# An expert layer's outputs: summed by matrix products in PSUM, or scattered to DRAM by row and gathered by token

## What is computed

```python
def hier_moe(h, router_grp, router_grp_b, router_exp, router_exp_b, w_gate, w_up, w_down):
    # top-1 group of 4, then top-2 experts of the 8 inside that group; 32 SwiGLU experts of width 256
    ...
    w_top = jax.nn.softmax(top_logit, axis=-1) * p_grp
    ...
    for grp in range(N_GROUPS):
        hid = silu(einsum('td,edf->tef', t, w_gate[grp])) * einsum('td,edf->tef', t, w_up[grp])
        out = out + einsum('tef,efd->td', hid * combine[:, grp, :, None], w_down[grp])

h_lat = h_lat + m_lat[5] * hier_moe(modulate(rmsnorm(h_lat, norm_ffn_g), ...), ...)
out = rmsnorm(h_lat, final_norm_g)
```

## Time and profile before

| | us |
|---|---|
| median of 3 runs | 2294.93 |
| the profiled execution's own time | 2294.58 |
| its span, first to last instruction | 2292.7 |
| PE busy in the span | 2112.8 (92%) |
| first matrix product of the pairs | at 1982.66 |
| end of the last combining product | at 2273.76 |
| mean granted TensorE clock | 0.953 of full |

### The profile page before, as it was taken

The page is one execution under the profiler, slowest core; times in us unless marked ns, Lnnn a source line. Parts: engine busy times, 40 slices in busy tenths (PEclk is TensorE's granted clock), DMA queues, the critical chain, the costliest instruction groups (busy, mean ns, idle before and its releaser), DMA issues. The chain is left out here.

```text
span 2292.7 us, 36330 instructions
## 1 busy us (share of the span) xinstructions
PE 2112.8 (92%) x15874; PEld 1296.2 (57%) x15874; DVE 798.8 (35%) x1625; ACT 512.7 (22%) x1042; POOL 101.1 (4%) x103
## 2 busy tenths in 40 slices
PE   6989999999999999999998887899988997799996
PEld 3545568854445658864544776885488643333332
DVE  1474323211185323310245446436344413311112
ACT  2223322201114413210121332123331201211111
POOL 0000000000000000000000011000012000000000
PEclk9999999999999999999998988899999998899998
DMA  6351325533343236334211000100110163298881
GB/s 260 146 201 56 145 110 220 221 147 147 127 187 139 104 124 257 147 147 155 92 43 51 3 3 2 48 13 37 74 40 3 45 258 131 97 391 349 351 347 59
DMA packets 30507, 313.87 MB, mean 137 GB/s; under 512 B 4744, under 2 KB 7184, under 8 KB 9488
## 3 DMA queue, kind: packets, MB, share of 16 engines
q1 hardware_dynamic: 28048, 308.40, 34.3%
q0 software_dynamic: 2304, 3.15, 0.4%
HBM read 330.39 MB, written 3.16 MB: 145 GB/s over the span
## 5 line engine op out<-in xcount | busy, mean ns | idle before, releaser
L511 ACT ACTIVATE arena<-pair 128x512 f32<-128x512 f32 (+5 forms) x339 | 181.0, 547 | 698.7 <-PE pair L885 170.6
L1262 PE MATMUL pair<-arena,weight_ring 128*128 128x256 f32 x1408 | 310.5, 383 | 2.9 <-ACT arena L785 2.9
L885 PE MATMUL pair<-weight_ring,arena 128*128 128x512 f32 (+1 forms) x640 | 277.0, 586 | 19.1 <-issue 11.3
L1262 PEld LDWEIGHTS pair<-arena,weight_ring 128*128 128x128 f32 x1408 | 269.7, 192 | 43.7 <-issue 6.8
L885 PEld LDWEIGHTS pair<-weight_ring,arena 128*128 128x128 f32 x640 | 122.9, 195 | 155.6 <-issue 150.1
L1308 PE MATMUL pair<-weight_ring,arena 128*128 128x512 f32 x352 | 151.5, 592 | 3.1 <-DVE arena L1282 3.1
L1282 DVE SCALAR_TENSOR_TENSOR arena<-pair,columns,arena 128x255 f32<-128x255 f32 (+1 forms) x176 | 76.7, 477 | 201.8 <-ACT arena L1273 200.3
L1308 PEld LDWEIGHTS pair<-weight_ring,arena 128*128 128x128 f32 x352 | 66.8, 190 | 86.7 <-issue 83.2
L1568 PEld LDWEIGHTS pair<-arena 64*64 64x64 f32 x3584 | 111.9, 140 | 4.4 <-issue 3.7
L1568 PE MATMUL pair<-arena 64*64 64x64 f32 x3584 | 113.8, 224 | 0.0
L1382 PE MATMUL pair<-weight_ring,arena 128*128 128x512 f32 (+1 forms) x256 | 106.5, 574 | 4.5 <-DVE arena L704 4.5
(11 more groups left out here) (473 smaller groups left out, 2642.1 us busy)
## 6 DMA issues: line engine op xcount, KB each, us to landing
weight_ring<-stream SPq DMA_DIRECT2D x85, 2048.0 KB, 7.4
weight_ring<-experts_in SPq DMA_DIRECT2D x17, 2048.0 KB, 10.3
arena<-experts_in SPq DMA_DIRECT2D x15, 2048.0 KB, 11.6
arena<-experts_out SPq DMA_DIRECT2D x8, 2048.0 KB, 14.3
weight_ring<-experts_out SPq DMA_DIRECT2D x8, 2048.0 KB, 13.2
weight_ring<-stream SPq DMA_DIRECT2D x4, 1024.0 KB, 4.8
arena<-rows_in SPq DMA_DIRECT2D x1, 3264.0 KB, 21.8
weight_ring<-stream SPq DMA_DIRECT2D x2, 1152.0 KB, 5.1
```

What stands on the lines that cost most here:

```text
L511: copy_act = lambda dst, src: nc.scalar.activation(dst, src, ACT_F.Copy)
L885: last = mm(bank[b][:, 0:n], hT[:, k, m * P:(m + 1) * P], w[:, k * n:k * n + n], start=(j == 0), stop=(j == KD - 1))
L1262: last = mm(bank[b][:, j * S:(j + 1) * S], w[:, at:at + P], hT[:, k, :], start=(k == 0), stop=(k == KD - 1))
```

## The change

The products with C and the factors spread over it are gone. A table `places_i` of row numbers is formed instead by DVE (`sorted_rows`), with one column for each pair and four columns for the tokens. ACT and DVE copy the down product out as before, without a factor, and POOL then scatters the 128 rows of Y, 4 KB each, to a DRAM tensor `y_dram` at their sorted places (`rows_out`). Slots with no row of work are sent to one of 16 spare rows if they lie on partitions 0 to 15, and out of bounds if not. Each scatter waits for the one before, and a Y buffer is written again once the scatter of two pairs earlier has landed. After the last scatter POOL gathers, for each of the two tiles of 128 tokens, the row of its first and of its second expert (four indirect DMAs of 512 KB). DVE multiplies them by gate factor and modulation row and adds them to the residual; then norm, gain and store run by tile. PSUM banks 2 to 5 take the down products in turn. The extra pairs move to places 5, 9, 13 and 17.

```diff
         starts_i = sb("window_starts", [P, 40], mybir.dt.int32)
+        places_i = sb("sorted_places", [P, 24], mybir.dt.uint32)
         rows_i = sb("extra_rows", [P, 8], mybir.dt.uint32)
         bias_dram = nc.dram_tensor("bias_rows", (HEADS, 2 * S - 1), F32, kind="Internal").ap()
+
+        y_dram = nc.dram_tensor("sorted_outputs", (2 * S + 16, D), F32, kind="Internal").ap()
 
...
             pair_windows = [2 * i for i in range(N_EXP // 2)]
-            for at, w in ((3, 32), (8, 34), (13, 36), (18, 38)):
+            for at, w in ((5, 32), (9, 34), (13, 36), (17, 38)):
...
-            for b, values, out_ in ((0, slots2, posT), (1, w12, wT)):
...
+            def sorted_rows():
+
+                link(tt(picked, taken_by, by_slot(ends), ALU.mult))
+                link(nc.vector.tensor_reduce(limits[:, N_EXP:N_EXP + 8], picked, AX, ALU.add))
+                nc.vector.tensor_copy(limits[:, 0:N_EXP], ends)
+                nc.vector.tensor_scalar(row_at[0:CH], firsts[0:CH, 0:40:2], k3c("slot", 1)[0:CH], None, ALU.add)
+                nc.vector.tensor_scalar(row_spare, k3c("slot", 1), k3c("skip", 1), 2.0 * S, ALU.subtract, ALU.add)
+                link(nc.vector.tensor_scalar(row_at[CH:P], firsts[CH:P, 1:40:2], k3c("slot", 1)[CH:P], -float(CH),
+                                             ALU.add, ALU.add))
+                tt(row_ok[0:CH], row_at[0:CH], limits[0:CH, 0:40:2], ALU.is_lt)
+                link(tt(row_ok[CH:P], row_at[CH:P], limits[CH:P, 1:40:2], ALU.is_lt))
+                link(nc.vector.scalar_tensor_tensor(row_at, row_at, row_spare, row_ok, ALU.subtract, ALU.mult))
+                link(nc.vector.tensor_scalar(row_at, row_at, row_spare, None, ALU.add))
+                nc.vector.tensor_copy(places_i[:, 0:20], row_at)
+                return nc.vector.tensor_copy(places_i[:, 20:24], place2.rearrange("p c m -> p (c m)"))
+            places_mark = dve_after(sorted_rows, ("dve", c.dve))
...
-            def combine_weights(i):
...
-                    link(nc.vector.scalar_tensor_tensor(parts_, posT, k3c("slot", 1, at), wT, ALU.is_equal, ALU.mult))
-                    tt(C, parts_[:, 0, :], parts_[:, 1, :], ALU.add).then_inc(dve_done, 1)
...
-                hT, Y = hTs[i % 2], Ys[i % 2]
+                hT, Y, ob = hTs[i % 2], Ys[i % 2], 2 + 2 * (i % 2)
                 if PE:
                     PE.wait_ge(act_done, hidden_done[i])
-                    if i >= 1:
-                        PE.wait_ge(act_done, left_done[i - 1])
-                        PE.wait_ge(dve_done, right_done[i - 1])
+                    if i >= 2:
+                        PE.wait_ge(act_done, left_done[i - 2])
+                        PE.wait_ge(dve_done, rows_done[i - 2])
                 w = await_expert(3 * i + 2)
...
-                                last = mm(bank[2 + h_][CH * j:CH * j + CH, :], hT[:, t, CH * j:CH * j + CH],
+                                last = mm(bank[ob + h_][CH * j:CH * j + CH, :], hT[:, t, CH * j:CH * j + CH],
...
                     if i >= 2:
-                        ACT.wait_ge(pe_done, combined[i - 2])
-                    nc.scalar.activation(Y[:, 0, :], bank[2][:, :], ACT_F.Copy).then_inc(act_done, 1)
+                        ACT.wait_ge(y_sent, 16 * (i - 1))
+                    copy_act(Y[:, 0, :], bank[ob][:, :]).then_inc(act_done, 1)
                 c.act += 1
                 left_done[i] = c.act
                 if DVE:
                     DVE.wait_ge(pe_done, outputs_done[i])
                     if i >= 2:
-                        DVE.wait_ge(pe_done, combined[i - 2])
-                    nc.vector.tensor_copy(Y[:, 1, :], bank[3][:, :]).then_inc(dve_done, 1)
+                        DVE.wait_ge(y_sent, 16 * (i - 1))
+                    nc.vector.tensor_copy(Y[:, 1, :], bank[ob + 1][:, :]).then_inc(dve_done, 1)
                 c.dve += 1
-                right_done[i] = c.dve
-
-            def combine(i):
-
-                C, Y = Cs[i % 2], Ys[i % 2]
-                if PE:
-                    PE.wait_ge(dve_done, max(weights_done[i], right_done[i]))
-                    PE.wait_ge(act_done, left_done[i])
-                    for m in range(TT):
-                        for h_ in range(2):
-                            last = mm(bank[4 + 2 * m + h_][:, :], C[:, P * m:P * m + P], Y[:, h_, :],
-                                      start=(i == 0), stop=(i == npairs - 1))
-                    last.then_inc(pe_done, 1)
-                c.pe += 1
-                combined[i] = c.pe
+                rows_done[i] = c.dve
+
+            def rows_out(i):
+
+                at = pair_windows[i] // 2
+                if POOL:
+                    POOL.wait_ge(dve_done, rows_done[i])
+                    POOL.wait_ge(act_done, left_done[i])
+                    if i:
+                        POOL.wait_ge(y_sent, 16 * i)
+                    POOL.indirect_dma_start(out=y_dram, out_offset=bass.IndirectOffsetOnAxis(ap=places_i[:, at:at + 1], axis=0),
+                                            in_=Ys[i % 2].rearrange("p a b -> p (a b)"), in_offset=None,
+                                            bounds_check=2 * S + 15, oob_is_err=False).then_inc(y_sent, 16)
 
             open_window(0)
             open_window(1)
-            for i in range(npairs + 2):
+            for i in range(npairs + 1):
                 if i < npairs:
                     expert_inputs(i)
                 if 1 <= i < npairs - 1:
                     open_window(i + 1)
                 if 1 <= i <= npairs:
                     hidden(i - 1)
-                if i >= 2:
-                    combine(i - 2)
-                if i < npairs:
-                    combine_weights(i)
                 if 1 <= i <= npairs:
                     expert_outputs(i - 1)
-            for b in range(4, 8):
-                bank_free[b] = None
-            for b in range(4, 8):
-                m, h = divmod(b - 4, 2)
-                read_out(b, fn_dve=lambda: link_first(lambda: add_gated(1, m, 512 * h, 512, bank[b][:, :])))
-
-            norm_rows(x[:, :, :], xn, TT)
-            for m in range(TT):
-                dve_step(lambda: tt(xn[:, m, :], xn[:, m, :], tail("fin", D), ALU.mult))
+                    rows_out(i - 1)
+            back = [sorted_x.rearrange("p a b -> p (a b)")[:, D * q:D * q + D] for q in range(4)]
+            if POOL:
+                POOL.wait_ge(act_done, window_copied[npairs - 1])
+                POOL.wait_ge(dve_done, places_mark[1])
+                POOL.wait_ge(y_sent, 16 * npairs)
+                for m in range(TT):
+                    for q in range(2):
+                        POOL.indirect_dma_start(
+                            out=back[2 * m + q], out_offset=None, in_=y_dram,
+                            in_offset=bass.IndirectOffsetOnAxis(ap=places_i[:, 20 + 2 * q + m:21 + 2 * q + m], axis=0),
+                            bounds_check=2 * S - 1, oob_is_err=False).then_inc(y_back[2 * m + q], 16)
+
+            root_ready = act_after(lambda: nc.scalar.activation(ss[:, 32:33], ss[:, 32:33], ACT_F.Sqrt), ("act", c.act))
+
+            def last_rows(m):
+                s1 = ss[:, m:m + 1]
+
+                def add_experts():
+                    first, second_ = back[2 * m], back[2 * m + 1]
+                    if DVE:
+                        DVE.wait_ge(y_back[2 * m], 16)
+                    link(nc.vector.scalar_tensor_tensor(first, first, w12[:, 0, m:m + 1], grow[:, 1, :], ALU.mult, ALU.mult))
+                    if DVE:
+                        DVE.wait_ge(y_back[2 * m + 1], 16)
+                    link(tt(x[:, m, :], x[:, m, :], first, ALU.add))
+                    link(nc.vector.scalar_tensor_tensor(second_, second_, w12[:, 1, m:m + 1], grow[:, 1, :], ALU.mult,
+                                                        ALU.mult))
+                    return tt(x[:, m, :], x[:, m, :], second_, ALU.add)
+                m_x = dve_after(add_experts)
+                yield
+
+                def squares():
+                    link(nc.scalar.activation(xn[:, m, :], x[:, m, :], ACT_F.Square, accum_out=s1))
+                    return copy_act(xn[:, m, 0:1], xn[:, m, 0:1])
+                a = act_after(squares, m_x, root_ready)
+                yield
+                d = dve_after(lambda: nc.vector.tensor_scalar(s1, s1, 1.0 / D, EPS, ALU.mult, ALU.add), a)
+                a = act_after(lambda: nc.scalar.activation(s1, s1, ACT_F.Sqrt), d)
+                yield
+
+                def scaled():
+                    link(nc.vector.reciprocal(s1, s1))
+                    return nc.vector.scalar_tensor_tensor(xn[:, m, :], x[:, m, :], s1, tail("fin", D), ALU.mult, ALU.mult)
+                d = dve_after(scaled, a)
+                if SP:
+                    SP.wait_ge(done[d[0]], d[1])
+                    SP.dma_start(out.rearrange("b (m p) d -> p (b m) d", p=P)[:, m, :], xn[:, m, :]).then_inc(stored, 16)
+                yield
+
+            together([last_rows(m) for m in range(TT)], [])
```

(4 more changed lines are left out.)

35 lines of the change are left out of this document (7 added, 28 removed).

## The result

The changed kernel took 2307.69 us, the median of 4 runs (2302.61 to 2312.55), against 2294.94 for the kernel before on the same chip (4 runs): a ratio of 1.0051, with a 95% interval of 1.0036 to 1.0065. It is slower, as forecast; the forecast was 2314. The profiled execution took 2302.61 us, the fastest of the four, and its span is 2300.7. So what the trace explains is +8.0 us of span (2292.7 to 2300.7), and the typical run lies 5 us above it.

What follows compares the result with a forecast made beforehand. PE bounded the stage with loads level; after the change loads and their slots would bind. Stage to 2283.0 plus an end of 29.2 gave span 2312.2, time 2314 us (chance 0.60), range 2289 to 2330.

Steps and rivals of the forecast that it cites:

- PE and the loads change places: Stage of the pairs: PE falls to 11.4 us a pair, loads need 14.85, so the loads bound it.
- What the slots allow: Stage: SP's queue idles at each extra pair until the inputs of the pair before it are done; faster PE doesn't help.
- Scatters: Stage: each scatter delays the loads on the same engines by 0.65 us, bounds 0 and 1.3.
- rival 2: Stage: scatters cost twice, 1.3 us, and extra loads their full 4.9; some 16 us more, 2330; chance 0.16.
- Extra loads: Stage: indirect loads of each extra pair delay SP's loads by 3.0 us, bounds 0 and 4.9.
- Cycles: Stage: four pairs, such as 6 to 10, including an extra pair, take 61.2 us against 57.1 before.
- the clock: Stage: each PE wait of over 2 us costs 1.7 us of lower clock, hidden where the queue is full.
- T: End of pair 19's outputs, closing the stage: 2283.0 on the profile's clock, against 2273.8 before.
- The end: From T to the span's end: copies, scatter, gathers, additions, norm and store take 29.2 us, 10.3 more than before.
- The start: First pair: ACT's window copies wait for `sorted_rows`, not the spread factors; inputs start 0.4 us earlier.
- Rival 1: Stage: loads at full rate, extra loads and scatters free, cycle 54.55 us; faster, 2285; chance 0.14.
- Rival 4: Stage: half of the two prices and no clock loss; nearly level, near 2296; chance 0.08.

Runs made afterwards that it cites:

- the halved loads: SP fetches half of each weight piece from the eighth on: changed kernel 2249.8 us, kernel before 2297.2 us, one run each.
- the old places: Changed kernel with extra pairs at places 3, 8, 13 and 18: 2301.7 us, 1.0013 of the kernel before.
- the three edits: Changed kernel, extra pairs at 3 to 6, first windows not waiting for the row table, end reordered by tile: 2294.3 us, 0.9991 of the kernel before.

## Why the prediction was right

**PE and the loads change places.** Shown, by the halved loads in both kernels. The 14.85 us for three pieces, taken from 424 GB/s, measured 14.8 without scatters. The waits forecast ahead of 13 pairs are there, 13 of them, 1.4 to 6.9 us each, and none inside extra pairs.

**What the slots allow.** Right: the queue pauses at each extra pair, and a faster PE did not shorten the pauses (39.9 us in all against 33.9 before). With them the 41 loads set a stage of 289.1 us where PE alone needs 231.6 and the loads at 4.95 us each some 203.

**Scatters.** 0.65 us was taken, 0.2 to 0.6 is measured. The doubled price of rival 2 did not occur. They landed up to 10.3 us after their issue, more than the 7.5 that was taken as the most, but under the 11 at which they would have held up POOL's queue, so nothing inside the stage waited for them.

**Extra loads.** This is the mis-sized term: 3.0 us for each extra pair, 12 in all, measured 4.3 in all. The step that failed is that two of the three pieces would now arrive while SP's queue is full. POOL issues these loads when the slots come free, and with PE waiting these came free later: pair 5's were issued from 2031.3 on, and SP's queue ran dry at 2035.5. Pair 4's pieces came 14.9 us after pair 3's and not 18.5. Of the packets of all extra loads 204 of 256 still fell into the pauses. How the others and the full loads gave way to each other is not shown.

**Cycles.** 61.2 us was forecast; the three of the profiled run are 58.1, 56.8 and 62.6 (pairs 6, 10, 14, 18). Besides the extra loads, the clock was charged too often: in the changed kernel's profile the products took 7.1 us behind waits of 1.4 to 2.0 us, and 8.6 us or more only behind those of 2.3 us and more. The rule of the prediction, 1.7 us for each wait of over 2 us, doesn't hold between runs either. In the changed kernel with the old places 7.1 us stand behind a wait of 2.56 us and 8.8 behind one of 2.11; in the stages of all profiles every wait of over 3.2 us lost the clock, but for the one ahead of the first pair with the three edits, which kept it behind 3.4. From pair 19 to the end it was 17.6, not 18.9, since the clock held. All this together put T at 2283.0, where it was 2272.7, 10.3 us too late. The last combining ended at 2273.8 before. So the stage, forecast as 9 us of the loss, gave about 1 back in this run, and 2 without the late start.

**The end.** 29.2 was forecast, 28.0 measured, by its parts: copies to the scatter's issue 0.9 forecast and 1.5 measured, scatter to the gather's issue 4.3 and 3.6, gather 4.8 and 4.4, additions 11.1 and 10.9 (with one wait of 0.8 for a gather in it), the rest 8.15 and 7.5. The scatter's landing, 2.6 us after its issue, lies under the 3.3 that was taken as the least. This term alone is +9.1 us, more than the profiled run lost in all. Measured from the last down product instead, which takes in the combining that was removed, it is 28.0 us against 23.4 before, and against 16.2 in the kernel before with its end cut by tile.

**The start.** Wrong in sign, though small: 0.4 us earlier forecast, 0.1 later measured from the end of the sorting products. I had counted DVE's instructions but not the 0.9 us between ACT's wait and its copy. The other 0.9 us of later start come from ahead of the stage.

So the mechanism held: the loads bound PE, and the end is a cost of its own. The sizes held less well. The profiled run lost 8.0 us where 19.5 were forecast, with nothing of it from the stage, so half of the forecast loss was not there, and that there is a loss at all rests on the end alone. That the median lies only 6 us under the forecast is partly luck: 5 of its 13 us of loss are outside the profiled run. Rival 1, at 2285, had the loads and slots right as well, and left out the scatters (6.9 us by the run without them), the extra loads (4.3) and the clock; its cycle of 54.55 us and the forecast's 61.2 stand on either side of the measured 59.2. Rival 4, with half of both prices, was nearest on the prices, but its 2296 left out the clock, which fell at eight waits inside the stage.

What stays open is the spread: the changed kernel's eight timed runs go from 2302.6 to 2316.6. Both of its profiles are of its fastest runs on their chips and agree to 0.2 us in stage and end, and what comes ahead of the stage ends up to 9 us apart over the profiles. So the spread may come from there, but no profile of a slower run of this kernel shows it.

## What to carry to other kernels

When an engine is 100% busy, read the DMA share and the longest landing beside it before pricing what its relief brings: here 0.99 and a load that landed as it was needed said that the freed TensorE time, worth 53 us with lighter loads, had nowhere to go. With loads issued on the release of slots, count also the stretches in which nothing is released: here 40 us of 289, a floor that neither bytes nor compute explain. And price a new round trip through DRAM at the end of a kernel by itself: from the last down product on, scatter, gather and unshared additions took 28.0 us, where the last combining and an end cut by tile took 16.2, in the place where nothing hides them.

## What the runs showed of the hardware

- 20 scatters of 128 rows, most of them dropped as out of bounds (616 rows of 4 KB moved in all), cost the loads 0.2 to 0.6 us each, but took 8.6 us (median) to land beside them, and 2.6 us with the queue empty.
- The page counts 13.65 MB written to HBM after and 3.16 before, a difference of 10.49 MB, which is 20 x 128 x 4 KB, dropped rows included. The packets of POOL's queue grew by only 4.63 MB (3.15 to 7.78), scatters and gathers together. The HBM figure of the page is not what was moved.
- A three-operand DVE form on 128x1024 took 1.28 us where twice the 128x512 row gave 1.5.
- Behind PE waits of 2.1 to 2.6 us the granted clock fell in some cases and not in others (32 products in 8.8 us behind 2.11, in 7.1 behind 2.56, in the same run), and behind 2.6 us ahead of the first pair it fell in three of four profiles of the kernel before and its variants.
- An ACT copy that needs a register read from SBUF began 0.9 us after what it waited for had ended (1981.14 to 1982.03); the copy of the last down product, which needs none, began within 0.1 us of its product's end (2272.74 to 2272.79).
